# w_out for the 32 sample tokens: three fp32r products in row blocks replaced by fp32 products on quarters of the array

## The reference, cut to what matters

```python
mix = jax.nn.sigmoid(ga) * y_a + jax.nn.sigmoid(gb) * y_b      # (tokens, 1024)
x = _layer_norm(ALPHA * x + mix @ w_out, ln1_g, ln1_b)         # w_out: 1024 x 1024
x = _layer_norm(ALPHA * x + _moe(x, w_router, ...), ln2_g, ln2_b)
```

## Time and profile before

| | us |
|---|---|
| median of 3 runs | 1023.2 |
| lowest and highest of the 3 | 1022.01, 1023.42 |
| the profiled execution | 1021.46 |
| its span, first to last instruction | 1020.3 |
| its mean granted clock | 0.933 |

### The profile page before, as it was taken

The page is one execution under the profiler, slowest core; times in us unless marked ns, Lnnn a source line. Parts: engine busy times, 40 slices in busy tenths (PEclk is TensorE's granted clock), DMA queues, the critical chain, the costliest instruction groups (busy, mean ns, idle before and its releaser), DMA issues.

```text
span 1020.3 us, 14646 instructions
## 1 busy us (share of the span) xinstructions
PE 889.7 (87%) x5949; PEld 806.3 (79%) x5949; DVE 606.3 (59%) x841; ACT 385.1 (38%) x382; POOL 101.5 (10%) x86
## 2 busy tenths in 40 slices
PE   6999999899998987999998996289889999999700
PEld 6999889788897987999998996268778888888600
DVE  3643453735556362033234245579999999999557
ACT  3521122121331313222222005157667787777301
POOL 3000000000000000101101011201011111110065
PEclk9989999999999989999999997589999999999955
DMA  9651360543606142122223612559899999999152
GB/s 284 211 207 42 94 206 1 176 124 94 206 1 183 55 130 89 42 83 84 83 91 130 281 63 108 185 186 319 315 382 400 421 412 414 415 415 393 67 175 87
DMA packets 79535, 195.26 MB, mean 191 GB/s; under 512 B 3889, under 2 KB 56841, under 8 KB 67192
## 3 DMA queue, kind: packets, MB, share of 16 engines
q1 hardware_dynamic: 72312, 168.88, 45.9%
q0 software_dynamic: 7168, 25.58, 6.6%
HBM read 167.65 MB, written 26.79 MB: 191 GB/s over the span
## 4 chain that ended last, share of the span: by engine, by line
PE 80%; DVE 13%; issue 3%; DMA 2%; ACT 2%; POOL 0%; POOLq 0%; SPq 0%; DVEq 0%; ACTq 0%
PE psum L419 23%; PE psum L421 22%; PE psum L420 22%; DVE split_lo L1354 2%; PE psum L1777 2%; PE psum L1796 2%; PE psum L1787 1%; PE psum L1995 1%; PE psum L1825 1%; DVE x L1623 1%; DMA xg<-x_rows,idx_i 1%; ACT split_hi L904 1%; DVE last_lo L1354 1%; PE psum L1811 1%; DVE onehot L1459 1%
## 5 line engine op out<-in xcount | busy, mean ns | idle before, releaser
L419 PE MATMUL psum<-x_hi,split_lo 128*128 128x272 f32 x704 | 212.0, 301 | 1.4 <-ACT ht L780 1.4
L421 PE MATMUL psum<-x_hi,split_hi 128*128 128x272 f32 x704 | 204.9, 291 | 0.0
L420 PE MATMUL psum<-x_lo,split_hi 128*128 128x272 f32 x704 | 204.8, 291 | 0.0
L1354 DVE TENSOR_TENSOR split_lo<-raw,split_hi 128x2048 fp32r<-128x2048 f32 x72 | 163.3, 2286 | 16.6 <-ACT split_hi L904 15.0
L414 DVE TENSOR_TENSOR split_lo<-raw,split_hi 128x2048 fp32r<-128x2048 f32 x35 | 80.1, 2290 | 137.1 <-ACT split_hi L395 136.9
L904 ACT CAST split_hi<-raw 128x2048 fp32r<-128x2048 f32 x72 | 137.5, 1913 | 54.3 <-PE psum L421 54.3
L419 PEld LDWEIGHTS psum<-x_hi,split_lo 128*128 128x128 f32 x704 | 135.6, 193 | 4.9 <-issue 2.7
L420 PEld LDWEIGHTS psum<-x_lo,split_hi 128*128 128x128 f32 x704 | 135.6, 193 | 1.5 <-issue 1.0
L421 PEld LDWEIGHTS psum<-x_hi,split_hi 128*128 128x128 f32 x704 | 135.3, 192 | 0.0
L395 ACT CAST split_hi<-raw 128x2048 fp32r<-128x2048 f32 x35 | 66.7, 1905 | 60.1 <-PE psum L421 58.4
L419 PE MATMUL psum<-split_hi,xgl 128*128 128x512 f32 x192 | 79.4, 414 | 2.8 <-DVE xgl L1515 2.8
(11 more groups left out here) (358 smaller groups left out, 1795.8 us busy)
## 6 DMA issues: line engine op xcount, KB each, us to landing
raw<-in_w_e_gate_dram SPq DMA_DIRECT2D x32, 1024.0 KB, 8.1
raw<-in_w_e_up_dram SPq DMA_DIRECT2D x32, 1024.0 KB, 7.9
raw<-in_w_e_down_dram SPq DMA_DIRECT2D x32, 1024.0 KB, 7.5
raw<-in_w_in_dram SPq DMA_DIRECT2D x26, 1024.0 KB, 7.0
cb<-in_state_C_dram SPq DMA_DIRECT2D x8, 1024.0 KB, 8.1
out_dram<-cb SPq DMA_DIRECT2D x8, 1024.0 KB, 5.9
y_slots<-ys POOLq DMA_DIRECT2D x16, 512.0 KB, 8.1
y_slots<-x_hi POOLq DMA_DIRECT2D x2, 2048.0 KB, 11.3
```

The source lines that it names most:

```text
L419: nc.tensor.matmul(out, a_lo, b_hi, start=first, stop=False)
L420: nc.tensor.matmul(out, a_hi, b_lo, start=False, stop=False)
L421: return nc.tensor.matmul(out, a_hi, b_hi, start=False, stop=last)
L1354: v.tensor_tensor(lo, raw2[:, n % MOE_SLOTS, :], hi.bitcast(F32), ALU.subtract).then_inc(w_lo, 1)
```

## The change

The unit WO 1 goes, and T 4 is no longer `rest_of_rows` but `sample_rows_of_out`. ACT keeps an unsplit fp32 copy of the 32 sample columns of each mix tile in a new tensor `mxs` (128 features x 8 x 32). For row block 4, PE multiplies `mxs` with the high part and with the low part of the weights, both read as plain fp32 (`bitcast(F32)`), two products instead of three. The stationary operand is 32 columns wide, and the result of column quarter q goes to PSUM partitions 32q to 32q + 31, all four to the same 256 columns of one bank. There are 8 steps x 2 parts x 4 quarters = 64 matmuls of 256 columns, with the four quarters innermost. DVE reads the result out in four additions of 32 x 256.

```diff
-    order += [("WO", 0), ("WO", 1)]
+    order += [("WO", 0)]
...
+    (mxs,) = lay(r_pool + XW * 4, r_mx, ("mxs", [P, KT, NS], F32))
...
         def mix_high(t):
             for c in range(2):
                 ac.wait_ge(mix_ok, 2 * t + c + 1)
+                nc.scalar.copy(mxs[:, 2 * t + c, :], sg[c][:, SEQ:N])
                 nc.scalar.copy(mxh[:, (2 * t + c) * N:(2 * t + c + 1) * N], sg[c][:]).then_inc(mxh_ok, 1)
...
+            else:
+                for q in range(4):
+                    cols = slice(256 * q, 256 * q + 256)
+                    last = v.scalar_tensor_tensor(x1[0:r, i, cols], x1[0:r, i, cols], ALPHA,
+                                                  wide(j)[q * NS:(q + 1) * NS, 0, 0:256], ALU.mult, ALU.add)
+            last.then_inc(z_free[j % 2], 1)
...
+        def sample_rows_of_out():
+
+            j = Z["T", PT]
+            z_room(pe, j)
+            pe.wait_ge(w_lo, C_WO + 4)
+            for k in range(KT):
+                for part in range(2):
+                    for q in range(4):
+                        w = chunk(C_WO + q, k, 0, 256)[part].bitcast(F32)
+                        last = mm(wide(j)[q * NS:(q + 1) * NS, 0, 0:256], mxs[:, k, :], w,
+                                  start=k == 0 and part == 0, stop=k == KT - 1 and part == 1)
             last.then_inc(z_done, 1)
```

More of the change, by code:

```diff
@@ L1361, in _ @@
         ve_.wait_ge(x1in, 16 * NT)
[L1362 to L1367, removed]
+        ve_.wait_ge(z_done, J_WO + 1)
+        v.scalar_tensor_tensor(x1[:, 0:PT, 0:256], x1[:, 0:PT, 0:256], ALPHA,
+                               wide(J_WO).rearrange("p b (q n) -> p (b q) n", q=2), ALU.mult, ALU.add
+                               ).then_inc(z_free[J_WO % 2], 1)
         def row_stats(i, var_sem):
@@ L1393, in _ @@
             ve_.wait_ge(z_done, j + 1)
-            v.scalar_tensor_tensor(x1[0:r, i, 256:DM], x1[0:r, i, 256:DM], ALPHA,
-                                   wide(j).rearrange("p b n -> p (b n)")[0:r, 0:DM - 256], ALU.mult, ALU.add
-                                   ).then_inc(z_free[j % 2], 1)
+            if i < PT:
+                last = v.scalar_tensor_tensor(x1[0:r, i, 256:DM], x1[0:r, i, 256:DM], ALPHA,
+                                              wide(j).rearrange("p b n -> p (b n)")[0:r, 0:DM - 256], ALU.mult, ALU.add)
+            else:
[4 more added lines that the diff above has]
+            last.then_inc(z_free[j % 2], 1)
             z_evacuated(ve_, J_WO)
-            z_evacuated(ve_, J_WO + 1)
             z_evacuated(ve_, j)
@@ L1923, in _ @@
         pe.wait_ge(w_lo, C_WO + 1)
[L1924 to L1930, removed]
+        z_room(pe, J_WO)
+        for i in range(PT):
+            last = out_rows(i, 0, wide(J_WO).rearrange("p b (q n) -> p (b q) n", q=2)[:, i, :])
+        last.then_inc(z_done, 1)
         def rest_of_rows(i):
@@ L1960, in _ @@
         for i in range(1, NT):
-            rest_of_rows(i)
+            if i < PT:
+                rest_of_rows(i)
+            else:
+                sample_rows_of_out()
             if i >= 2:
```

## The result

| | before | changed |
|---|---|---|
| median of 8 runs, us | 1022.56 | 1015.63 |
| lowest and highest, us | 1018.32, 1023.74 | 1013.83, 1019.4 |
| span of the profiled execution, us | 1020.3 | 1014.1 |

The ratio is 0.994, with a 95% interval of 0.9919 to 0.9962: 6.1 us faster, between 3.9 and 8.3. The direction was forecast. So the question was where 2 us more came from, or whether they are the change's at all.

What follows compares the result with a forecast made beforehand. PE alone was taken to bound the kernel from w_out to XT 3. On PE -11.4 + 7.2, on ACT +0.1, gave -4.1 us; taken from the runs' median, 1019.1 us, range 1016.8 to 1021.8.

Steps and rivals of the forecast that it cites:

- The bound: From w_out to XT 3, PE alone sets the pace: busy 61.27 of 61.44 us at clock 1.00.
- What goes and comes on PE: Row block 4 of w_out: 96 matmuls go, -11.4 us; 64 matmuls on quarters come, +7.2 us.
- the sum: Over the whole kernel: -11.4 and +7.2 us on PE, +0.1 us on ACT, giving -4.1 us.
- a change of 0.13 us at each end: At both ends of T 4, PE's switch between quarters and the full array: 0.13 us each, besides 32 rounds of 0.22.
- The burst L1811: Existing 16 matmuls on quarters, 1.96 us, used to price T 4: 0.22 us a round.
- ACT: Before w_out: of eight small copies seven are hidden, the last delays the last cast, +0.1 us.
- DVE: T 4's read-out becomes four additions, +0.75 us over 0.94, at no cost behind ACT's splits.
- That weight loads are not hidden: Rival in T 4: each round costs stream and load, 0.33 us, T 4 10.6 us; total 1022.5 us, 4%.
- The fall of the clock in T 4: Rival: quarters let PE's clock fall to half, T 4 takes 14 us; +5.4 us, 1028.6 us, 6%.
- The one-after-the-other case: Rival in T 4: quarters run in turn, 28 us, +17 us; total 1040 us, 2%.
- what moves the sum without the change: The clock at the experts' start: a later rise could lose up to 1.7 us; it could hardly come sooner.
- The base: The whole kernel before the change: the median of three runs, 1023.2 us, from which 4.1 us was taken.

Runs made afterwards that it cites:

- its double: The changed kernel with T 4's products of the sample rows done twice, 64 rounds instead of 32: 1025.28 us, ratio to the kernel before 1.0027.
- the 75: The kernel before, unedited: its own 12 runs and those beside the other sets, mean 1022.4 us, standard deviation 2.0.
- the larger sets: 24 later runs of the unedited changed kernel, mean 1018.3 us, and 75 runs of the unedited kernel before, mean 1022.4 us.
- the kernel without T 4: The changed kernel with two of T 4's 32 rounds left, so sample outputs lack w_out: 1014.84 and 1013.13 us; mean of all 11 runs 1014.2.

## Why the prediction was right and wrong

The bound, right: PE sets the pace from w_out to XT 3, and its time there goes to the end; 6.9 us more work on it cost 6.9 us by the medians and 7.2 by the means, with a standard error of 0.9.

What goes and comes on PE, right. Compared at the same clock, w_out to XT 3 is 62.34 against 66.5 us without a half-clock stretch, and 63.84 against 68.03 with one: -4.2 us both times, where the sum has -11.4 + 7.2 = -4.2. T 4's 7.04 us and the 0.2 us more in logits 2 make the 7.2. The sum splits it otherwise, with a change of 0.13 us at each end, so that part came out right only as a total. The burst L1811 was the right row to price it by: four such bursts with their tails would have been 7.8.

ACT, right: +0.12 us. DVE, right: 1.70 us instead of 0.94, hidden by ACT's splits. The prediction had DVE done with row block 4 some 7.5 us after T 4's end, though its own terms, 5.7 and 0.75, give 6.5; it was 6.5 (622.75 against 616.22), and ACT was free for XT 4 only at 625.47.

The rivals. That weight loads are not hidden is refuted by the rounds of 0.22 us, in each of which four loads of 0.11 us take place on the same rows: they overlap the matmuls and one another. Here the trace does not agree with the rule of the Trainium skill ("TensorE: Matmul & The Clock Gate", Packing small matmuls) weighed in the prediction, that loads overlap matmuls in flight only on another group of rows: 32 rounds took 7.04 us. The fall of the clock in T 4 is refuted by both T 4 and its double. The one-after-the-other case exists, but only if the program orders it so.

What failed is the step on what moves the sum without the change, and with it the range; the mechanism and the sum held. I wrote that the clock could take away up to 1.7 us at the experts' start and could "hardly come sooner", looked at that stretch alone, and drew the range narrow below and wide above. Yet the earlier trace rows has a second stretch at 0.50 in the path, at w_out's start, and that one could be missing: it was, in the profile, for 1.5 us. And for the scatter of runs I took the 1.4 us between three runs, where it is a standard deviation of 2.0 us, 9 us from lowest to highest over all runs of the kernel before. The difference of two sets of 8 then has a standard error of 1 us by their means. The first 8 runs of the changed kernel lay on the short side of this scatter: six of them at a mean clock of 0.934 or more, where a quarter of the later ones were. The ends of the range do not follow from the terms named for it either: these give 1017.3 and 1022.9, where it says 1016.8 and 1021.8. With the sum unchanged, 1.5 us for the stretch and 2 us for the scatter would have put the lower end at 1019.1 - 3.5 = 1015.6 (an estimate that may count the clock twice), which is just what was measured.

The base was off too, by 0.8 us in the same direction: the three runs gave 1023.2, the 75 give 1022.4. By the larger sets the changed kernel stands at 1018.3, inside the range.

So the size was right and the first comparison lay off it: over 24 and 75 runs the change is worth 4.1 us, 0.4%. What stays open is why six of the first 8 runs had the higher clock, and why the kernel without T 4 gives 1.4 us back.

## What to carry to other kernels

Where few tokens meet wide weights, put each quarter of the columns on its own quarter of the array and let the quarters alternate matmul by matmul; here an fp32 product in two parts then beat three fp32r products on a block that is three quarters padding, by 4.1 us, but in the other order of loops it lost by 14. Price such a form by the distance of starts inside a burst of the same form, not by its busy time divided by its count. And before stating a range, compare what the profile's own chance events (each half-clock stretch on the path, in either direction) and many runs of the unchanged kernel say of the scatter: three runs say little. And compare the mean clock of the runs on both sides before an odd difference is put down to the change.

## What the runs showed of the hardware

One quarter of the array at work alone takes 0.197 us for a recorded pass of 256 fp32 columns with 32 stationary ones, four side by side 0.22 us: 3.6 times as much work in the time.

Quarters in a row kept the granted clock at 1.00: for 13.95 us with four in turn, for 25.24 us with one after the other.

In code that differs up to there by ACT's small copies alone, the start of w_out lies between 555.9 and 560.1 us in ten profiled executions that have PE's rest ahead of it, and the rest of 3.0 to 3.1 us is followed by a half-clock stretch in eight of them and by none in two. The same rest, the same work before it: whether it costs 1.5 us differs from one execution to the next.
